# Two attention stages of a one-core transformer kernel: value products moved into free columns of the score banks, two banks left to turned pieces alone, and the inversion of the sums issued ahead of the next maximum

## What is computed

```python
def gqa_sink_attend(qb, keys, vals, bias, sink_g):      # first block, "window": 256 context keys + a band of 3 x 128
    s = jnp.einsum('bqkgd,bskd->bkgqs', qb, keys, ...) * (DH_A ** -0.5)
    ...
    p = jax.nn.softmax(jnp.concatenate([s, s_sink], axis=-1), axis=-1)[..., :-1]
    o = jnp.einsum('bkgqs,bskd->bqkgd', p.astype(vals.dtype), vals)
...
def chunk_band_attention(q, k, v, rel_table):           # second block, "band": up to 9 chunks of 64 keys, bias by distance
    ...
        s = jnp.einsum('bqhd,bkhd->bhqk', qc, kc).astype(jnp.float32) * scale + bias
        ...
        p = jax.nn.softmax(s, axis=-1).astype(v.dtype)
        return jnp.einsum('bhqk,bkhd->bqhd', p, vc)
```

## Time and profile before

| | us |
|---|---|
| time, median of 3 runs | 3230.39 (3229.07 to 3231.68) |
| profiled execution, span from first to last instruction | 3229.0 |
| PE busy over the span | 3059.6 (95%) |
| DVE, ACT, POOL busy | 1504.1, 816.7, 833.4 |
| window stage, about 252 to 395 us into the span: PE, DVE, ACT, POOL busy | 129.80, 84.31, 90.71, 75.48 |
| band stage, about 1927 to 2047: PE, DVE, ACT, POOL busy | 105.05, 64.11, 76.51, 61.97 |

### The profile page before, as it was taken

One profiled execution on the slowest core, in us unless ns is written; L12 is line 12 of the kernel. 1 busy time (PEld: TensorE's weight loads), 2 busy tenths in 40 slices (PEclk: granted clock), 3 DMA queues, 4 the chain that ended last, 5 costly groups with the idle time before them and its releaser, 6 DMA issues. The chain is left out here.

```text
span 3229.0 us, 37151 instructions
## 1 busy us (share of the span) xinstructions
PE 3059.6 (95%) x14618; PEld 1737.2 (54%) x14618; DVE 1504.1 (47%) x2490; ACT 816.7 (25%) x1658; POOL 833.4 (26%) x659
## 2 busy tenths in 40 slices
PE   7999999999949999799999998899998999999999
PEld 4447756666424444344456656444445666665444
DVE  2216537676451111524322465413767777775224
ACT  3126524443211111412211126211011222221001
POOL 0004401012100010023023215422626655561323
PEclk9999999999979999899999999999999999999999
DMA  7210000001277897511000130011221221117544
GB/s 295 78 52 29 2 1 27 1 27 55 79 312 305 334 341 261 181 39 39 30 24 28 54 137 2 20 52 60 90 80 44 79 78 73 71 52 272 173 128 137
DMA packets 72316, 334.58 MB, mean 104 GB/s; under 512 B 10960, under 2 KB 12496, under 8 KB 58320
## 3 DMA queue, kind: packets, MB, share of 16 engines
q1 hardware_dynamic: 67536, 315.42, 25.8%
q0 software_dynamic: 4608, 16.78, 2.1%
HBM read 283.92 MB, written 48.23 MB: 103 GB/s over the span
## 5 line engine op out<-in xcount | busy, mean ns | idle before, releaser
L3366 PE MATMUL banks<-down_ring,down_sums 128*128 128x512 f32 x440 | 192.2, 599 | 3.6 <-DVE down_ring L3393 3.6
L835 PE MATMUL banks<-kT_b,qT_b_and_w_out 96*128 96x512 f32 (+1 forms) x384 | 158.8, 523 | 3.6 <-ACT prob_b L897 2.4
L3068 PE MATMUL banks<-hT,ffn_raw 128*128 128x512 f32 x352 | 156.5, 598 | 2.4 <-PEq L2554 1.3
L330 PE MATMUL banks<-w_in,hT 128*128 128x512 f32 (+1 forms) x384 | 157.5, 567 | 1.2 <-PEq L157 1.2
L728 POOL TENSOR_TENSOR prob<-prob,softmax_columns 128x640 f32<-128x640 f32 (+1 forms) x64 | 75.5, 1201 | 314.6 <-DVE softmax_columns L686 314.6
L3184 DVE SCALAR_TENSOR_TENSOR ffn_acc<-ffn_u,s_ffn_taps,ffn_acc 128x1023 f32<-128x1023 f32 x88 | 131.6, 1506 | 30.4 <-ACT ffn_acc L3121 28.8
L3366 PEld LDWEIGHTS banks<-down_ring,down_sums 128*128 128x128 f32 x440 | 84.6, 192 | 110.8 <-issue 104.7
L1789 PE MATMUL banks<-hT,side_ring 128*128 128x512 f32 x256 | 127.5, 617 | 1.3 <-PEq L2341 1.3
L1436 PE MATMUL banks<-expert_wg,expert_xT 128*128 128x512 f32 x256 | 114.7, 602 | 2.4 <-ACT expert_xT L1473 1.7
L330 PEld LDWEIGHTS banks<-w_in,hT 128*128 128x128 f32 x384 | 71.8, 190 | 81.8 <-issue 78.5
L1452 PE MATMUL banks<-expert_wd,expert_hT 128*128 128x512 f32 x256 | 112.6, 593 | 1.2 <-DVE expert_y L1507 1.2
(11 more groups left out here) (624 smaller groups left out, 6108.0 us busy)
## 6 DMA issues: line engine op xcount, KB each, us to landing
down_ring<-in_w_down SPq DMA_DIRECT2D x132, 256.0 KB, 2.9
expert_wg<-in_w_gate SPq DMA_DIRECT2D x16, 2048.0 KB, 15.1
expert_wu<-in_w_up SPq DMA_DIRECT2D x16, 2048.0 KB, 20.9
expert_wd<-in_w_down SPq DMA_DIRECT2D x16, 2048.0 KB, 8.5
ffn_raw<-in_w_ffn SPq DMA_DIRECT2D x22, 1024.0 KB, 6.4
wmod_slab<-in_w_mod SPq DMA_DIRECT2D x6, 2048.0 KB, 8.0
act_rows<-ffn_acc SPq DMA_DIRECT2D x22, 512.0 KB, 2.7
act_rows<-act_rows SPq DMA_DIRECT2D x22, 512.0 KB, 8.1
```

The source lines that it names most:

```text
L330: last = nc.tensor.matmul(c.ps[:, base + a:base + b], h[:, q, :], k.w_in[i][:, q, 0:b - a], start=q == 0, stop=q == KD - 1)
L835: last = nc.tensor.matmul(scores(u)[:, a:b], heads[u // 2].q[u % 2], heads[u // 2].keys[u % 2][:, a:b], start=True, stop=True, skip_group_ ...
L3068: last = nc.tensor.matmul(c.bank(fi), wt[:, q, :], x[:, q, :], start=q == 0 and m != 2, stop=q == 3, skip_group_check=True)
L3366: return nc.tensor.matmul(c.bank(4 * (p % 2) + t), stationary_of(s)[:, P * t:P * t + P], w[s % RING][:, 0, :], start=j == 0, stop=j == N - 1)
```

## The change

It has three parts, all in `attend_pairs`, and an order of keys at the two places that call it.

- **Products.** The product of v goes to columns 640 to 767 of the middle bank of set v % 2. It now waits for DVE's copy of product v-2, and for what empties this set of scores: in the window stage the exponentials of pair v+2, in the band stage its maximum. The scores of a 5-tile pair that fall into the middle bank wait for the copy of the product of u-4. The keys are put in an order in which the middle bank is written third and not first.
- **Turned pieces.** Banks 6 and 7 alternate between pieces alone: a piece waits for the piece two before it.
- **Inverse.** On DVE the inverse of u-1 is issued ahead of the maximum of u, and no longer behind it.

```diff
@@ attend_pairs
-    freed, use_of_piece, use_of_product = [], {}, {}
...
+    done_of = [((out_act, out_dve)[by_engine], count) for _, _, _, by_engine, count in pieces]
 
     def product(v):
-        return c.bank(TURN + use_of_product[v] % 2, P)
+        at = SET * BANK * (v % 2) + 5 * P
+        return c.ps[:, at:at + P]
 
     def turn_bank(g, m):
-        at = BANK * (TURN + use_of_piece[g] % 2)
+        at = BANK * (TURN + g % 2)
         return c.ps[:, at:at + m]
...
-                    if use_of_piece[g] >= 2:
-                        pe.wait_ge(*freed[use_of_piece[g] - 2])
+                    if g >= 2:
+                        pe.wait_ge(*done_of[g - 2])
...
                         bank = (e * second(u) + a) // BANK
+                        if bank == 1 and e == 0 and u >= 4:
+                            pe.wait_ge(taken, u - 3)
...
-                    if use_of_product[v] >= 2:
-                        pe.wait_ge(*freed[use_of_product[v] - 2])
+                    if v >= 2:
+                        pe.wait_ge(taken, v - 1)
+                    if s + 1 < n:
+                        pe.wait_ge(exped if pre is None else negmax, 2 * (s + 2) if pre is None else s + 2)
...
             for s in range(-2, n + 1):
                 u = s + 2
+                if 0 < u <= n:
+                    inverse(u - 1)
                 if u < n:
...
                         nc.vector.tensor_scalar(st[:, 1, :], st[:, 0, :], -1.0, None, ALU.mult).then_inc(negmax, 1)
-                    if u:
-                        inverse(u - 1)
-                if u == n:
-                    inverse(n - 1)
                 if s >= 1:
@@ window stage, 5 tiles
-                keys = [(0, 2 * BANK // 2, band[0][:, 2 * P:3 * P]), (1, CTX, band[1]), (0, 0, ctx[0]), (1, P, ctx[1][:, P:CTX]),
+                keys = [(0, 0, ctx[0]), (1, CTX, band[1]), (0, BANK, band[0][:, 2 * P:3 * P]), (1, P, ctx[1][:, P:CTX]),
@@ band stage, 5 tiles
-                cuts = [(0, 512, 640), (1, 128, 384), (0, 0, 256), (1, 384, 640), (0, 256, 512), (1, 0, 128)]
+                cuts = [(0, 0, 256), (1, 128, 384), (0, 512, 640), (1, 384, 640), (0, 256, 512), (1, 0, 128)]
```

## The result

| | time, median | ratio to before (95% interval) | span profiled | window stage | band stage |
|---|---|---|---|---|---|
| before | 3229.73 (3229.07 to 3231.68, 4 runs) | | 3229.0 | 141.1 | 118.4 |
| changed | 3252.07 (3249.60 to 3252.46, 4 runs) | 1.0069 (1.0056 to 1.0081) | 3250.7 | 157.7 | 124.3 |

The kernel before has one run more here than in the table ahead of the prediction, hence 3229.73 and not 3230.39. Forecast: 3254, between 3238 and 3268, slower with a chance of 0.90. A stage is counted here, and in all that follows, from the start of its first maximum to the end of its last copy of a product on DVE, in the profiled execution: 253.37 to 394.51 us and 1928.06 to 2046.43 before. The span grew by 21.7 us, the two stages by 16.6 + 5.9 = 22.5; the rest of the kernel, which is not touched, is 0.8 shorter in sum.

What follows compares the result with a forecast made beforehand. PE was taken to set the pace before; after the change, a ring through DVE operations blocked by POOL. Window stage +17.4 and band stage +6 made 23.4 us on 3230.4, so 3254, between 3238 and 3268.

Steps and rivals of the forecast that it cites:

- a ring through a block behind POOL: Both stages: inverse, small DVE operations held until POOL ends, ACT's exponentials, next inverse; 4.95 us window, 4.52 us band.
- Its size in the window stage: Window stage: +17.4 us, with 147.7 us from first maximum to last against 130.3 before.
- The 5-tile step: Window stage: 4.95 us for a 5-tile pair against 4.52 before, or 3.97 without the block.
- one wrong price: Window stage, 4-tile maximum behind a 5-tile pair: L697 slips between POOL's operations, L698 is held; step of 4.73 us.
- a price of 0.14 more for each step: Skill page's reading: L697's whole 0.16 us follows POOL's end; 8 us more over some 55 steps, 3262.
- The rival of a block up to the end of POOL's first operation: Window ring of 4.0 to 4.3 us, stage +3, band stage 0, total 3233: no measurable change; chance 0.04.
- PE's new waits, the third rival: Late product copy brings the third score product into the ring: 0.3 us on some 45 pairs, +14, 3268; chance 0.05.
- The band stage: Band stage: +6 us, bounds +1 and +12, from 5-tile pairs +7.1, smaller pairs -2.4 and first round +1.
- A round's four smaller pairs: Band stage: 12.81 us now, estimated 11.5; half the difference taken, -0.6 a round, -2.4 in all.
- The rest of the change: Banks and key order: PE's 6.6 us wait for ACT's piece goes but buys nothing; PE's new waits are hidden.
- PE's share in the window stage: Window stage: PE's busy share falls from 91% to about 80%.
- The rival that it would be faster: Both stages: overlap doesn't block, PE stays the bound and loses its waits; together -12 us, 3218; chance 0.06.

Runs made afterwards that it cites:

- e1: The changed kernel with the inverse of u-1 back behind the maximum of u on DVE, products still in the score banks: 3220.6 us, ratio 0.9965.
- e3: The changed kernel with POOL multiplying only one column of each head, all waits kept, outputs not the reference's: 3211.4 us, ratio 0.9943.
- e4: The changed kernel, complete, with DVE's small operations remade so none has two SBUF inputs or is a TENSOR_SCALAR: 3209.72 us, ratio 0.9932.
- e2: The kernel before with only the inverse of u-1 moved ahead of the maximum, products still in banks 6 and 7: 3255.65 us, ratio 1.0074.
- e10: The changed kernel with POOL filling each head's probabilities with a constant twice instead of multiplying, outputs not the reference's: 3212.97 us, ratio 0.9950.

## Why the prediction was right

- **That the moved inverse closes a ring through a block behind POOL.** Right, shown from four sides: without the move (e1), without POOL's work (e3) and without the blockable operations (e4) the loss is gone, and with the move alone (e2) it is all there.
- **Its size in the window stage.** +17.4 forecast, +16.6 measured; maxima over 147.7 against 146.7. The 5-tile step was right to 0.01 or 0.02 us, from a single case in the trace of before. Of the 1.0 us too much between the first maximum and the last, 0.6 is one wrong price, used three times: where a 4-tile maximum follows a 5-tile pair, L695 slips in between POOL's two operations and L696 is held, as forecast (the 1177 ns of its row). But the held L696 ends with POOL, and not 0.20 behind it, so this step takes 4.53 us and not 4.73 (L681 at 285.70 and 290.23). That case also decided rightly against a price of 0.14 more for each step: L695 ends 0.02 behind POOL's end, not 0.16. One of its supports was misread: the earlier trace rows show durations, and the L3184 of 2.32 us (from 2513.12) ends at 2515.44, where no POOL operation ends. The matching ends are those of rows 7 and 9.
- **The rival of a block up to the end of POOL's first operation.** It falls: L695 ends behind the second at 27 of the 31 pairs at which POOL works. PE's new waits, the third rival, never held up a maximum of the window stage either: DVE stood idle for scores once, 1.8 us, ahead of the first.
- **The band stage.** +6 forecast, +5.9 measured. A 5-tile step was 4.53 us (forecast 4.52). A round's four smaller pairs were estimated more than read: 12.2 us forecast, half-way between 12.8 and 11.5, and 12.02 measured. The first round was put 2.3 us longer and is 3.9 longer. So part of this agreement is luck. And the gain in the smaller pairs was put down to the moved inverse, when e2, which has it alone, doesn't show it: it comes from the score banks.
- **The rest of the change.** That it gives nothing while the ring binds was right in the window stage (157.2 in e2, 157.7 here) and wrong in the band stage, where it gives 3.2 us. "The new order of keys has the same widths" doesn't mean that it is free: the twelve score records of a 5-tile pair take 1.48 us in the new order (e4) and 1.36 in the old (first e4, then the kernel before; in the changed kernel the ring hides it):

```profile
300.69 1.48 PE L630 MATMUL banks<-kT_a,qT_a 64*128 64x256 f32 x12
```

```profile
304.17 1.36 PE L636 MATMUL banks<-kT_a,qT_a 64*128 64x128 f32 x12
```

  And I named the wrong wait. I expected PE to wait for the exponentials ahead of its product; the chain of waits has 4.9 us of that in the window stage, while PE stands idle 7.6 us at the third score product for the copy of a product, and 11.5 us in the band stage. The changed kernel's row for the window stage:

```profile
PE banks L630 <- DVE OT L712: 7.6, 18, 1.0
```

  The copy stands behind the blocked operation on DVE. It stayed off the ring: DVE never stood idle for scores in the 5-tile steps shown.
- **PE's share in the window stage.** I expected about 80% busy; it is 89%, 141.53 of 159 us against 129.80 of 143, with the same instructions. A small part of that is the clock. Busy time by stretch in the fill of the changed kernel (columns as in the earlier trace rows, the granted clock is the third from the end):

```profile
258.00:264.00 6.00, 4.39 (x31) 3.67 (x31) 4.01 (x8) 2.73 (x7) 3.46 (x3) 0.78 0.13 56
264.00:270.00 6.00, 4.21 (x37) 3.02 (x36) 3.69 (x8) 3.61 (x11) 2.46 (x2) 0.93 0.00 0
270.00:276.00 6.00, 5.76 (x59) 4.37 (x58) 3.70 (x8) 3.70 (x10) 2.46 (x2) 1.00 0.01 3
```

  Behind two stops of PE, 1.54 and 1.34 us for exponentials, the clock is at 1.2 in place of 2.4 GHz for part of these stretches; it was at 1.00 through the whole stage before. It costs nothing here, since the ring binds: from 261.03 to 265.96 the inverse's step is 4.93 us, as later. Most of the rest lies where PE stops ahead of the third score product. The twelve score records of such a pair take 0.92 and, behind the stop, 1.03 us, 1.95 in all, against 1.36 before; 18 such stops make an estimated 10.6 of the 11.7 us:

```profile
305.96 0.92 PE L630 MATMUL banks<-kT_a,qT_a 64*128 64x256 f32 x4
...
307.33 1.03 PE L630 MATMUL banks<-kT_a,qT_a 64*128 64x128 f32 x8 [0.46 <-DVE OT L712]
```

  The lesson is that a busy PE said nothing about what bounds this stage.
- **The rival that it would be faster.** The trace spoke against it, and e3 and e4 show what it would have been worth: I put the unblocked kernel at 3218, and it is 3210 to 3211. The step that fell short is the value of the banks and the early inverse in the band stage: -4 forecast, -6.2 measured (e4); in the window stage it is 9.1 for 7.8. What remains is in the untouched parts, and its cause isn't shown.

## What to carry to other kernels

Before an instruction is moved earlier in an in-order queue, ask what its new start sets off on other engines, and what will then run beside it. Here two operations of 0.16 us each cost nothing only because POOL was idle when they ran. A single case of the overlap in the trace of before (one operation of 1.13 us in place of 0.16, ending with POOL's) was enough to price it. The cure was not to undo the order but to take the small operations out of POOL's way (one input from PSUM, a negation by a reduction, the sink's difference formed on ACT), which turned 0.69% slower into 0.68% faster.

## What the runs showed of the hardware

- A DVE operation on two columns with both inputs in SBUF takes as long as what is left of the POOL multiplication (SBUF to SBUF) beside it (1.12 for 0.16 us, changed kernel), and ends up to 0.02 us behind it. With one input in PSUM it takes 0.156 us under the same work (e4). A TENSOR_REDUCE from SBUF to SBUF (two columns, 154 to 156 ns at all 32 pairs of e4's band stage, POOL at work at 28 of them) is not held either, and there replaces a TENSOR_SCALAR as a negation.
- POOL's MEMSET over the same columns does not hold an operation with two SBUF inputs, but does hold a TENSOR_SCALAR (e10: the first took 160 to 163 ns, the second 378 in the median and up to 600, where 170 is its time alone).
